# A two-layer attention trunk on one core: the product with the values turned round, with value pairs stationary, the transposed probabilities moving, and three float32r passes

## The chip, the core and the metric

The kernel runs on one core of a Trainium2 chip. The metric is the device time of one execution, in microseconds (us). Three runs of the kernel before took 888.66 to 889.86 us, with a median of 889.16 us.

## The reference, cut to what matters

The program is two layers over a sequence of 256 positions and 1024 columns. Each layer is a token mixer of three attention branches in parallel, followed by a SwiGLU network, each with a residual and a layer norm. The change touches only the last product of the three attentions:

```
p = softmax(logits)                       # per head: 256 queries x 256 keys, causal
o = p @ v                                 # v: 256 x 64 per head
ya, yb, yc: heads merged                  # 384, 256 and 384 columns
merged = sum_b gate_b * (y_b @ w_b)       # w_pa, w_pb, w_pc
```

The branches have 6, 4 and 6 heads here. The middle one is the dilated attention. It has three patterns of 4 heads, whose logits share one softmax for each of the 4 key-value heads, so that its probabilities are 3 groups that are added before the product with the values.

## The kernel before, in words

**Operands.** Everything is float32 in memory. For the large products each operand is split into a high part, rounded to float32r, and a low part, the rest, and the product is three passes: high by high, high by low, low by high. Weights arrive in pieces of up to 128x2048 in `raw`. ACT writes `w_hi` (L760) and DVE writes `w_lo` (L856). Activations are transposed by PE through an identity matrix, and ACT and DVE write the high and low part of the transposed tile out of PSUM (L764 and L861).

**One plan, five engines.** `write_plan` writes out one list of steps by hand. Every engine walks the whole list in order and issues its share of each step, so the order of the list is the order of each engine's queue. A weight product step is `mm` (L1040), 12 matmuls on a piece of 4 blocks. In the attention part, `attend` puts one half of an attention step behind each `mm`.

**Attention steps.** A unit is one pair of heads and one tile `t` of 128 queries. A layer has 16 units, in the order branch, pair, tile. `tick` k plans, in this order, the sum of the three groups of unit k-1 on POOL if that is dilated (L733, L734), the transposition of the probabilities of unit k-2 (`turn_p`, L1119, with ACT's copy to `prob_t` at L819), and the scores of unit k (L1099). DVE masks the scores and takes the maximum (L910 and L914), and ACT does the exponentials with their sums (L813). `half_tick` k, one `mm` later, plans the third group of scores of a dilated unit with t = 1 (`scores2`, L1099, L926) and the product with the values of unit k-2:

```
for e in range(2):
    h = 2 * u["p"] + e
    for j in range(u["t"] + 1):
        ins = pe.matmul(out[:, e * HEAD_DIM:(e + 1) * HEAD_DIM],
                        prob_t[:, e * w + j * P:e * w + (j + 1) * P],
                        values[g % 2][:, j, h * HEAD_DIM:(h + 1) * HEAD_DIM],
                        start=j == 0, stop=j == u["t"])
```

The transposed probabilities are stationary there, and 64 columns of values move (L1131), in plain float32. DVE then multiplies by the reciprocal of the sums and writes `y` (L934, L935). When a branch is complete, PE transposes `y` (L1055), and ACT and DVE split it for the projection `proj`.

**Queries, keys, values.** The step `spread` (L781) copies a finished block of the input product out of PSUM, on ACT: queries and keys to `stage`, values to `values`. For two branches POOL rotates the staged part (rope, L723 to L726) before PE transposes it (`turn_qk`, L1065). The forget gates of the first branch (`forget`, L877 to L890) need the third block, and `forget_sum` (L1075) on PE waits for them. Small transposed tiles alternate between two PSUM banks (`aux_bank`).

## Time and profile before

| | |
|---|---|
| median of 3 runs | 889.16 us |
| the profiled execution: its time | 889.12 us |
| its span | 887.3 us |
| PE busy | 842.2 us (95% of the span) |
| DVE busy | 511.1 us (58%) |
| ACT busy | 401.6 us (45%) |
| POOL busy | 48.9 us (6%) |
| chain that ended last | PE 84%, DVE 7%, ACT 3%, DMA 2%, POOL 2%, issue 1% |

The profile is of one execution. PE, DVE, ACT and POOL are the engines, PEld is PE's load of the stationary operand. In the trace's rows the first number is the start, the second the duration, both in us. Matmuls overlap one another, so what one costs is read from the distance of the starts. A float32 matmul leaves two records and a float32r matmul or a transposition one. The row of a stretch gives the stretch and its length, then PE, PEld, DVE, ACT and POOL busy with the number of instructions, PE's granted clock, the DMA share and GB/s. The row of a group gives its count, busy us and mean ns, then its idle time before it. A bracket at the end of a row is the time for which the engine sat idle before it, and what ended that.

### The profile page before, as it was taken

Reading aid. Unit: us, or ns where it says so; the run is one execution under the profiler, and the core shown is the slowest. Engines: PE = TensorE matmul, PEld = TensorE weight load, DVE = VectorE, ACT = ScalarE, POOL = GpSimd, SP = SyncE. Lnnn points to the kernel's source line nnn. Section 1 sums busy time; section 2 is a strip of 40 time slices with the busy share of each in tenths; the row PEclk is TensorE's granted clock in tenths of the full one; section 3 lists DMA queues with packets and bytes.
Section 4 is the critical chain, followed back from the end, with each engine's and each line's share of the span. In section 5 each row is a group of like instructions: output and inputs, shape, how many; then the busy total and the mean of one; then the engine's idle time right before and its main releaser. Section 6 shows DMA issues by size and latency. Waiting matters only on the chain.

```text
span 887.3 us, 10728 instructions
## 1 busy us (share of the span) xinstructions
PE 842.2 (95%) x4216; PEld 696.1 (78%) x4216; DVE 511.1 (58%) x728; ACT 401.6 (45%) x536; POOL 48.9 (6%) x86
## 2 busy tenths in 40 slices
PE   3989999999998999999999899999999899999995
PEld 2867888888886888888878678888888688888884
DVE  6564454636787545445685535554858765445436
ACT  3565455544444444344337554654444354344330
POOL 0012151000000000000000222300000000000000
PEclk9999999999999999999999999999999999999998
DMA  9573424456546864664437342434663675665601
GB/s 321 167 243 110 143 72 146 140 188 221 192 135 205 260 194 158 208 194 160 153 108 236 120 143 83 135 127 154 210 220 118 234 237 190 190 190 177 202 0 49
DMA packets 93458, 149.35 MB, mean 168 GB/s; under 512 B 3424, under 2 KB 52832, under 8 KB 93408
## 3 DMA queue, kind: packets, MB, share of 16 engines
q1 hardware_dynamic: 93408, 148.66, 51.4%
q8 instruction: 35, 0.57, 0.3%
q14 instruction: 15, 0.12, 0.0%
HBM read 147.60 MB, written 1.05 MB: 168 GB/s over the span
## 4 chain that ended last, share of the span: by engine, by line
PE 84%; DVE 7%; ACT 3%; DMA 2%; POOL 2%; issue 1%; SPq 0%; POOLq 0%; ACTq 0%; DVEq 0%
PE bank L1040 74%; PE bank L1055 3%; PE bank L1099 3%; DVE w_lo L856 2%; DMA raw<-in_w_in 2%; PE bank L1131 2%; ACT w_hi L760 1%; PE bank L1119 1%; PE bank L1065 1%; POOL rope_cos L723 1%; ACT shared L813 1%; DVE stats L973 1%; DVE x L1006 1%; DVE x L970 1%; DVE x L1003 1%
## 5 line engine op out<-in xcount | busy, mean ns | idle before, releaser
L856 DVE TENSOR_TENSOR w_lo<-raw,w_hi 128x2048 fp32r<-128x2048 f32 (+3 forms) x142 | 307.6, 2171 | 88.9 <-ACT w_hi L760 88.5
L1040 PE MATMUL bank<-w_hi,act_hi 128*128 128x512 f32 (+2 forms) x864 | 343.1, 397 | 3.4 <-DVE act_lo L861 3.4
L1040 PE MATMUL bank<-w_hi,act_lo 128*128 128x512 f32 (+2 forms) x864 | 333.5, 386 | 0.0
L1040 PE MATMUL bank<-w_lo,act_hi 128*128 128x512 f32 (+2 forms) x864 | 332.3, 385 | 0.0
L760 ACT CAST w_hi<-raw 128x2048 fp32r<-128x2048 f32 (+3 forms) x142 | 257.5, 1814 | 146.7 <-PE bank L1040 122.6
L1040 PEld LDWEIGHTS bank<-w_hi,act_hi 128*128 128x128 f32 x864 | 163.3, 189 | 33.0 <-DVE act_lo L861 3.8
L1040 PEld LDWEIGHTS bank<-w_hi,act_lo 128*128 128x128 f32 x864 | 162.8, 188 | 32.9
L1040 PEld LDWEIGHTS bank<-w_lo,act_hi 128*128 128x128 f32 x864 | 163.4, 189 | 28.7
L1040 PE MATMUL bank<-w_hi,y_hi 128*128 128x512 f32 x240 | 95.2, 397 | 0.0
L1040 PE MATMUL bank<-w_hi,y_lo 128*128 128x512 f32 x240 | 93.7, 391 | 0.0
L1040 PE MATMUL bank<-w_lo,y_hi 128*128 128x512 f32 x240 | 93.6, 390 | 0.0
L861 DVE TENSOR_TENSOR y_lo<-bank,y_hi 128x256 fp32r<-128x256 f32 (+1 forms) x56 | 23.3, 440 | 57.2 <-ACT y_hi L764 57.2
L1040 PEld LDWEIGHTS bank<-w_hi,y_lo 128*128 128x128 f32 x240 | 45.1, 188 | 9.5
L764 ACT CAST y_hi<-bank 128x256 fp32r<-128x256 f32 (+1 forms) x56 | 20.0, 387 | 71.9 <-PE bank L1055 71.9
L1040 PEld LDWEIGHTS bank<-w_hi,y_hi 128*128 128x128 f32 x240 | 45.1, 188 | 9.2
L1040 PEld LDWEIGHTS bank<-w_lo,y_hi 128*128 128x128 f32 x240 | 45.2, 188 | 8.8
L958 DVE TENSOR_TENSOR act_fn<-act_fn,bank 128x256 f32<-128x256 f32 x44 | 18.5, 421 | 58.2 <-ACT act_fn L829 56.5
L813 ACT ACTIVATE shared<-shared,neg_max 128x128 f32<-128x128 f32 (+3 forms) x64 | 33.8, 529 | 31.1 <-DVE neg_max L926 15.9
L829 ACT ACTIVATE act_fn<-bank 128x256 f32<-128x256 f32 x44 | 16.9, 384 | 61.8 <-PE bank L1040 61.8
L914 DVE CUSTOM_DVE_ANT_0 shared<-bank,tables 128x128 f32<-128x128 f32 (+1 forms) x48 | 15.3, 355 | 50.8 <-PE bank L1107 26.8
L723 POOL TENSOR_TENSOR rope_cos<-stage,tables 128x128 f32<-128x128 f32 (+1 forms) x16 | 11.3, 706 | 491.6 <-ACT stage L781 491.6
L869 DVE TENSOR_TENSOR qk_lo<-bank,qk_hi 128x512 fp32r<-128x512 f32 (+1 forms) x24 | 14.4, 602 | 41.4 <-ACT qk_hi L787 41.4
(88 smaller groups left out, 533.4 us busy)
## 6 DMA issues: line engine op xcount, KB each, us to landing
raw<-in_w_in SPq DMA_DIRECT2D x48, 1024.0 KB, 5.2
raw<-in_w_gate SPq DMA_DIRECT2D x44, 512.0 KB, 3.9
raw<-in_w_up SPq DMA_DIRECT2D x44, 512.0 KB, 5.0
raw<-in_w_down SPq DMA_DIRECT2D x22, 1024.0 KB, 5.0
raw<-in_w_o SPq DMA_DIRECT2D x8, 1024.0 KB, 5.3
raw<-in_w_in SPq DMA_DIRECT2D x4, 768.0 KB, 4.4
raw<-in_w_pa SPq DMA_DIRECT2D x4, 768.0 KB, 4.4
raw<-in_w_pc SPq DMA_DIRECT2D x4, 768.0 KB, 4.5
```

The source lines that it names most:

```text
L723: link(pool.tensor_tensor(rc, v, c4, ALU.mult))
L760: act.copy(weights(w_hi, i, HI_SLOTS), weights(raw, i, RAW_SLOTS)).then_inc(hi_done, 1)
L764: act.copy(hi[dst][:, dk:dk + nk, t * P:(t + 1) * P], group_view(bank[b], nk, P)).then_inc(turn_hi, 1)
L813: act.activation(pr, pr, ACT.Exp, bias=neg_max[:, slot:slot + 1], scale=-1.0, accum_out=denom[:, slot:slot + 1]).then_inc(exp_done, 1)
L829: act.activation(act_fn[2 * (c % 2) + t][:, 0:256], bank[b][:, 0:256], ACT.Silu).then_inc(silu_done, 1)
L856: dve.tensor_tensor(weights(w_lo, i, HI_SLOTS), weights(raw, i, RAW_SLOTS), weights(w_hi, i, HI_SLOTS).bitcast(F32), ALU.subtract).then_in ...
L861: dve.tensor_tensor(lo[dst][:, dk:dk + nk, t * P:(t + 1) * P], group_view(bank[b], nk, P), hi[dst][:, dk:dk + nk, t * P:(t + 1) * P].bitca ...
L958: dve.tensor_tensor(a[:, 256:512], a[:, 0:256], bank[b][:, 256:512], ALU.mult).then_inc(drained[b], 1)
L1040: ins = pe.matmul(bank[use[0]][:, 0:width], a, w[:, k, c0:c0 + width], start=start and k == 0 and p == 0, stop=stop and k == nk - 1 and p ...
L1055: ins = pe.transpose(out[:, k * P:(k + 1) * P], source(src, buf, k0 + k, t), ident)
L1099: ins = pe.matmul(bank[b][:, off:off + w], a[g % 2][rows, q, t * P:(t + 1) * P], k[g % 2][rows, K_PAIR[br] + pair, 0:w], start=p == 0, sto ...
L1131: ins = pe.matmul(out[:, e * HEAD_DIM:(e + 1) * HEAD_DIM], prob_t[:, e * w + j * P:e * w + (j + 1) * P], values[g % 2][:, j, h * HEAD_DIM: ...
```

## The change

The product with the values is planned once for a pair of heads, at its tile t = 1, and not once for each tile. The values of both heads (128 columns) are stationary, and the transposed probabilities of both heads and both tiles move: 512 columns for the first block of keys and 256 for the second. Values and probabilities are split into high and low parts, with three float32r passes for each block. The result comes out transposed, with both heads' values against both heads' probabilities. The two halves that belong together (`own_blocks`) are copied to `y_hi` by ACT and `y_lo` by DVE. The transposition of `y` goes away.

For this there are new steps. A step `weigh` on DVE, in the half tick behind the unit's exponentials, takes the reciprocal of the sums and multiplies the probabilities in place, and PE's `turn_p` now waits for it. DVE writes `prob_t_lo` in `turn_p`, ahead of the maxima of the same tick, and releases that bank. DVE writes `v_lo` in `spread`. Buffers of queries, keys and values are chosen by branch and not in rotation. The diff, cut to its core:

```
 PAIRS = [h // 2 for h in BRANCH_HEADS]
+ACT_SLOTS = [[0, 1, 2, 3], [4, 5, 6, 7]]
+Y_SLOTS = [[0, 1, 2], [3, 4], [5, 0, 1]]
                 plan.append(("sum", stage_of[k - 1]))
             if 0 <= k - 2 < len(units):
                 d = stage_of[k - 2]
-                d["pt"] = aux_bank()
+                d["pt"], d["pt_n"] = aux_bank(), count.next("pt")
...
             k = tick_at[0] - 1
             if 0 <= k < len(units) and stage_of[k]["b"] == 1 and stage_of[k]["t"]:
                 stage_of[k]["s2"] = [bank(4), bank(5)]
-                plan.append(("scores2", stage_of[k], g0 + 1))
-            if 0 <= k - 2 < len(units):
+                plan.append(("scores2", stage_of[k]))
+            if 0 <= k - 1 < len(units):
+                plan.append(("weigh", stage_of[k - 1]))
+            if 0 <= k - 2 < len(units) and stage_of[k - 2]["t"] == TT - 1:
                 d = stage_of[k - 2]
                 d["o"] = aux_bank()
-                plan.append(("values", d, g0 + d["b"]))
-                if d["p"] == PAIRS[d["b"]] - 1:
-                    last_y[d["b"], d["t"]] = d["o"]
-                    y_due.append((d["b"], d["t"]))
-
-        y_due = []
-        last_y = {}
+                plan.append(("values", d, count.next("values")))
+                for t in range(TT):
+                    y_turned[d["b"], t] = d["o"]
+
...
-            for b, t in due:
-                y_turned[b, t] = turn("y", 0, 0, BRANCH_KT[b], t, "y", 3 * ((g0 + b) % 2),
-                                      ("bank", last_y[b, t]))
-                    ev = dict(e=staged[0], b=b, pair=first, np=width // P, t=t, rope=b > 0, g=g0 + b, col=col)
-            plan.append(("spread", layer, c, t, use, segs, ev, g0))
+                    ev = dict(e=staged[0], b=b, pair=first, np=width // P, t=t, rope=b > 0)
+            v_n = count.next("v") if any(seg[0] == "v" for seg in segs) else 0
+            plan.append(("spread", c, t, use, segs, ev, v_n))
+            if c == 2:
+                forget_from[0] = v_n
             if ev is not None:
+                ev["staged"] = ("v", v_n) if v_n else ("bank", use)
...
-        values = [sb(f"values{s}", [P, TT, 384]) for s in range(2)]
+        shapes = [("ac", 384, 6), ("b", 256, 8)]
+        v_hi, v_lo = ([sb(f"v_{part}_{n}", [P, TT, width], F32R) for n, width, _ in shapes] for part in ("hi", "lo"))
-        prob_t = sb("prob_t", [P, 2 * SEQ])
-        y = sb("y", [P, TT, 384])
+        prob_t_hi, prob_t_lo = (sb(f"prob_t_{part}", [P, 3, 2 * P], F32R) for part in ("hi", "lo"))
...
+        def own_blocks(o):
+
+            return [(slice(e * HEAD_DIM, (e + 1) * HEAD_DIM),
+                     o[e * HEAD_DIM:(e + 1) * HEAD_DIM, :].rearrange("p (t e q) -> p t e q", t=TT, e=2)[:, :, e, :])
+                    for e in range(2)]
...
                         elif what == "v":
-                            out = values[(g0 + br) % 2][:, t, first:first + width]
+                            out = v_hi[br % 2][:, t, first:first + width]
                         ins = act.copy(out, src)
-                    ins.then_inc(drained[b], 1)
+                    ins.then_inc(v_hi_done if v_n else drained[b], 1)
...
                     u = step[1]
                     b, n = u["pt"]
                     act.wait_ge(filled[b], n)
-                    act.copy(prob_t[:, 0:2 * u["w"]], bank[b][:, 0:2 * u["w"]]).then_inc(drained[b], 1)
+                    t = u["t"]
+                    act.copy(prob_t_hi[:, t:2 * t + 1, :], group_view(bank[b], t + 1, 2 * P)
+                             ).then_inc(prob_t_hi_done, 1)
+                elif kind == "values":
+                    _, u, _ = step
+                    b, n = u["o"]
+                    act.wait_ge(filled[b], n)
+                    for rows, own_block in own_blocks(bank[b]):
+                        ins = act.copy(hi["y"][rows, Y_SLOTS[u["b"]][u["p"]], :].rearrange("p (t q) -> p t q", t=TT),
+                                       own_block)
+                    ins.then_inc(y_hi_done, 1)
...
                                       ALU.subtract).then_inc(drained[b], 1)
+                elif kind == "spread" and step[6]:
+                    _, c, t, (b, n), segs, ev, v_n = step
+                    dve.wait_ge(v_hi_done, v_n)
+                    for what, br, first, col0, width in segs:
+                        if what == "v":
+                            dve.tensor_tensor(v_lo[br % 2][:, t, first:first + width], bank[b][:, col0:col0 + width],
+                                              v_hi[br % 2][:, t, first:first + width].bitcast(F32),
+                                              ALU.subtract).then_inc(drained[b], 1)
                 elif kind == "forget":
 
-                    _, layer, (fb, fn) = step
+                    _, layer, v_n = step
                     dve.wait_ge(tables_loaded, 48)
-                    dve.wait_ge(drained[fb], fn)
+                    dve.wait_ge(v_hi_done, v_n)
                     link(dve.tensor_tensor(f_in[:, :, :], f_in[:, :, :],
...
                                                  dil_mask[:, 2, :], -SCALE, nm, ALU.add, ALU.min,
                                                  nm).then_inc(drained[b], 1)
+                elif kind == "weigh":
+
+                    u = step[1]
+                    s0 = 2 * (u["u"] % 4)
+                    if u["b"] == 1:
+                        dve.wait_ge(summed, u["sum_n"])
+                    else:
+                        dve.wait_ge(exp_done, 2 * u["u"] + 2)
+                    link(dve.reciprocal(rdenom[:, s0:s0 + 2], denom[:, s0:s0 + 2]))
+                    for e in range(2):
+                        pr = prob[u["t"]][e][:, 0:u["w"]]
+                        ins = dve.tensor_scalar(pr, pr, rdenom[:, s0 + e:s0 + e + 1], None, ALU.mult)
+                    ins.then_inc(weighed, 1)
+                elif kind == "turn_p":
+                    u = step[1]
+                    b, n = u["pt"]
+                    t = u["t"]
+                    dve.wait_ge(prob_t_hi_done, u["pt_n"])
+                    dve.tensor_tensor(prob_t_lo[:, t:2 * t + 1, :], group_view(bank[b], t + 1, 2 * P),
+                                      prob_t_hi[:, t:2 * t + 1, :].bitcast(F32),
+                                      ALU.subtract).then_inc(drained[b], 1)
                 elif kind == "values":
-                    u = step[1]
+                    _, u, y_n = step
                     b, n = u["o"]
-                    s0, h0 = 2 * (u["u"] % 4), 2 * u["p"] * HEAD_DIM
-                    dve.wait_ge(filled[b], n)
-                    link(dve.reciprocal(rdenom[:, s0:s0 + 2], denom[:, s0:s0 + 2]))
-                    dve.tensor_tensor(y[:, u["t"], h0:h0 + 2 * HEAD_DIM].rearrange("p (e c) -> p e c", e=2),
-                                      group_view(bank[b], 2, HEAD_DIM),
-                                      rdenom[:, s0:s0 + 2].unsqueeze(2).broadcast_to([P, 2, HEAD_DIM]),
-                                      ALU.mult).then_inc(drained[b], 1)
+                    k = Y_SLOTS[u["b"]][u["p"]]
+                    dve.wait_ge(y_hi_done, y_n)
+                    for rows, own_block in own_blocks(bank[b]):
+                        by_t = [m["y"][rows, k, :].rearrange("p (t q) -> p t q", t=TT) for m in (lo, hi)]
+                        ins = dve.tensor_tensor(by_t[0], own_block, by_t[1].bitcast(F32), ALU.subtract)
+                    ins.then_inc(drained[b], 1)
...
                 elif kind == "turn_p":
                     u = step[1]
-                    if u["b"] == 1:
-                        pe.wait_ge(summed, u["sum_n"])
-                    else:
-                        pe.wait_ge(exp_done, 2 * u["u"] + 2)
+                    pe.wait_ge(weighed, u["u"] + 1)
-                    w = u["w"]
-                    for e in range(2):
-                        for j in range(u["t"] + 1):
-                            ins = pe.transpose(out[:, e * w + j * P:e * w + (j + 1) * P],
-                                               prob[u["t"]][e][:, j * P:(j + 1) * P], ident)
+                    for j in range(u["t"] + 1):
+                        for e in range(2):
+                            c0 = (2 * j + e) * P
+                            ins = pe.transpose(out[:, c0:c0 + P], prob[u["t"]][e][:, j * P:(j + 1) * P], ident)
                     ins.then_inc(done, 1)
                 elif kind == "values":
-                    _, u, g = step
+
+                    _, u, _ = step
                     pb_, pn = u["pt"]
                     pe.wait_ge(drained[pb_], pn)
                     out, done = take(u["o"])
-                    w = u["w"]
-                    for e in range(2):
-                        h = 2 * u["p"] + e
-                        for j in range(u["t"] + 1):
-                            ins = pe.matmul(out[:, e * HEAD_DIM:(e + 1) * HEAD_DIM],
-                                            prob_t[:, e * w + j * P:e * w + (j + 1) * P],
-                                            values[g % 2][:, j, h * HEAD_DIM:(h + 1) * HEAD_DIM],
-                                            start=j == 0, stop=j == u["t"])
+                    pair = slice(u["p"] * P, (u["p"] + 1) * P)
+                    for j in range(TT):
+                        cols = slice(j * 2 * P, 4 * P)
+                        for p, (v, pt) in enumerate(((v_hi, prob_t_hi), (v_hi, prob_t_lo), (v_lo, prob_t_hi))):
+                            moving = pt[:, 2 * j:2 + j, :].rearrange("p a q -> p (a q)")
+                            ins = pe.matmul(out[:, cols], v[u["b"] % 2][:, j, pair], moving,
+                                            start=j == 0 and p == 0, stop=j == TT - 1 and p == 2)
                     ins.then_inc(done, 1)
```

The first place is DVE's queue in the middle of the dilated branch. Units are counted from 0 in a layer: unit 5 is the first branch's last, units 6 and 7 are the dilated pair 0 at t = 0 and t = 1, and unit 8 is pair 1 at t = 0. Before, from behind the third group's maxima of unit 7 (`scores2`) to behind the `w_lo` after the maxima of unit 8:

```order
L934 RECIPROCAL rdenom<-denom 128x2 [waits filled6]
L935 TENSOR_TENSOR y<-bank,rdenom 128x128 [waits dve_own]
L910 ISA shared,neg_max<-bank,tables 128x384 [waits filled4]
L910 ISA shared,neg_max<-bank,tables 128x384 [waits filled5]
L861 TENSOR_TENSOR y_lo<-bank,y_hi 128x3x128 [waits turn_hi]
L856 TENSOR_TENSOR w_lo<-raw,w_hi 128x2048 [waits hi_done]
L934 RECIPROCAL rdenom<-denom 128x2 [waits filled7]
L935 TENSOR_TENSOR y<-bank,rdenom 128x128 [waits dve_own]
```

The same stretch now, up to the `weigh` of unit 7 (the last two rows), for which the `turn_p` of unit 7 waits on PE:

```order
L971 RECIPROCAL rdenom<-denom 128x2 [waits summed]
L974 TENSOR_SCALAR shared<-shared,rdenom 128x128 [waits dve_own]
L991 TENSOR_TENSOR y_lo<-bank,y_hi 64x256 [waits y_hi_done]
L991 TENSOR_TENSOR y_lo<-bank,y_hi 64x256
L981 TENSOR_TENSOR prob_t_lo<-bank,prob_t_hi 128x256 [waits prob_t_hi_done]
L944 ISA shared,neg_max<-bank,tables 128x384 [waits filled4]
L944 ISA shared,neg_max<-bank,tables 128x384 [waits filled5]
L903 TENSOR_TENSOR v_lo_ac<-bank,v_hi_ac 128x384 [waits v_hi_done]
L882 TENSOR_TENSOR w_lo<-raw,w_hi 128x2048 [waits hi_done]
L971 RECIPROCAL rdenom<-denom 128x2 [waits summed]
L974 TENSOR_SCALAR shared<-shared,rdenom 128x256 [waits dve_own]
L974 TENSOR_SCALAR shared<-shared,rdenom 128x256
```

In the new queue there stand `y_lo` of unit 5, `prob_t_lo` of unit 6 and `v_lo`, and each waits for ACT. The maxima of unit 8 and a `w_lo` of 2048 stand behind them and ahead of the `weigh` of unit 7. The reciprocal and multiply behind the product, and `y_lo` of a transposition, are gone.

ACT's queue over the same stretch, before, from the exponentials of unit 7:

```order
L813 ACTIVATE shared,denom<-shared,neg_max 128x768 [waits drained4]
L813 ACTIVATE shared,denom<-shared,neg_max 128x768 [waits drained5]
L760 CAST w_hi<-raw 128x2048 [waits piece_used,raw_full1]
L819 COPY prob_t<-bank 128x256 [waits filled7]
L813 ACTIVATE shared,denom<-shared,neg_max 128x384 [waits drained4]
L813 ACTIVATE shared,denom<-shared,neg_max 128x384 [waits drained5]
L764 CAST y_hi<-bank 128x3x128 [waits filled6]
L781 COPY values<-bank 128x384 [waits filled2]
L781 COPY values<-bank 128x384 [waits filled3]
```

And now:

```order
L829 ACTIVATE shared,denom<-shared,neg_max 128x768 [waits drained4]
L829 ACTIVATE shared,denom<-shared,neg_max 128x768 [waits drained5]
L843 CAST y_hi<-bank 64x256 [waits filled6]
L843 CAST y_hi<-bank 64x256
L776 CAST w_hi<-raw 128x2048 [waits piece_used,raw_full1]
L836 CAST prob_t_hi<-bank 128x256 [waits filled7]
L829 ACTIVATE shared,denom<-shared,neg_max 128x384 [waits drained4]
L829 ACTIVATE shared,denom<-shared,neg_max 128x384 [waits drained5]
L797 CAST v_hi_ac<-bank 128x384 [waits filled2]
L797 CAST v_hi_ac<-bank 128x384 [waits filled3]
```

ACT has the same work here but for `y_hi`: it stands ahead of the piece's `w_hi` and in two parts, where it stood behind the exponentials of unit 8 in one. The copy of the probabilities still stands behind that `w_hi`. DVE's `prob_t_lo` now waits for this copy.

## Rows read from the trace of the kernel before

**Rows 1.** Busy time by engine in the attention part of layer 1 (windows)
```profile
63.00:196.00 133.00, 128.64 (x753) 106.74 (x751) 64.67 (x135) 68.20 (x126) 24.03 (x40) 1.00 0.40 127
```
**Rows 2.** Groups by line, PE: the transpositions of the staged queries and keys
```profile
L1065 PE MATMUL bank<-tables,stage 128*128 128x128 f32 x80 | 13.5, 283 | 8.7 <-POOL stage L726 8.7
```

**Rows 3.** Timeline, PE: the product with the values of a unit with t = 1
```profile
151.84 0.39 PE L1040 MATMUL bank<-w_hi,act_lo 128*128 128x512 f32 x1
152.07 1.00 PE L1131 MATMUL bank<-values,prob_t 128*128 128x64 f32 x8
...
153.19 0.39 PE L1040 MATMUL bank<-w_lo,act_hi 128*128 128x512 f32 x1
```

**Rows 4.** Timeline, PE: float32r matmuls of 256 columns; a transposition of y
```profile
56.15 0.28 PE L1075 MATMUL bank<-upper_r,logf_lo 128*128 128x256 f32 x1
56.27 0.22 PE L1077 MATMUL bank<-upper_r,logf_hi 128*128 128x128 f32 x1
...
195.20 0.39 PE L1040 MATMUL bank<-w_hi,act_lo 128*128 128x512 f32 x1
195.44 0.49 PE L1055 MATMUL bank<-tables,y 128*128 128x128 f32 x3
...
196.00 0.39 PE L1040 MATMUL bank<-w_lo,act_hi 128*128 128x512 f32 x1
```

**Rows 5.** Timeline, PE: the longest staged wait, and turn_p of unit 7
```profile
114.56 0.66 PE L1065 MATMUL bank<-tables,stage 128*128 128x128 f32 x4 [1.62 <-POOL stage L726]
...
132.40 0.60 PE L1119 MATMUL bank<-tables,shared 128*128 128x128 f32 x4
```

**Rows 6.** Timeline, DVE: from the third maxima of unit 7
```profile
123.19 0.48 DVE L926 CUSTOM_DVE_ANT_0 shared<-bank,tables,neg_max 128x256 f32<-128x256 f32 x1
...
126.81 0.56 DVE L910 CUSTOM_DVE_ANT_1 shared<-bank,tables 128x384 f32<-128x384 f32 x1 [2.34 <-PE bank L1099]
...
129.32 0.56 DVE L861 TENSOR_TENSOR y_lo<-bank,y_hi 128x384 fp32r<-128x384 f32 x1 [1.46 <-ACT y_hi L764]
129.79 2.28 DVE L856 TENSOR_TENSOR w_lo<-raw,w_hi 128x2048 fp32r<-128x2048 f32 x1
131.99 0.16 DVE L934 RECIPROCAL rdenom<-denom 128x2 f32<-128x2 f32 x1
132.18 0.29 DVE L935 TENSOR_TENSOR y<-bank,rdenom 128x128 f32<-128x128 f32 x1
```

**Rows 7.** Timeline, ACT: the same stretch
```profile
123.70 0.94 ACT L813 ACTIVATE shared<-shared,neg_max 128x768 f32<-128x768 f32 x1 [3.51 <-DVE neg_max L926]
...
125.56 1.89 ACT L760 CAST w_hi<-raw 128x2048 fp32r<-128x2048 f32 x1
127.35 0.36 ACT L819 COPY prob_t<-bank 128x256 f32<-128x256 f32 x1
127.61 0.61 ACT L813 ACTIVATE shared<-shared,neg_max 128x384 f32<-128x384 f32 x1
...
128.82 0.46 ACT L764 CAST y_hi<-bank 128x384 fp32r<-128x384 f32 x1
129.18 0.85 ACT L781 COPY values<-bank 128x384 f32<-128x384 f32 x2
```

**Rows 8.** Timeline, DVE and POOL: the forget gates' start; two POOL additions
```profile
50.22 0.42 DVE L869 TENSOR_TENSOR qk_lo<-bank,qk_hi 128x256 fp32r<-128x256 f32 x1 [0.89 <-ACT qk_hi L787]
50.56 2.28 DVE L856 TENSOR_TENSOR w_lo<-raw,w_hi 128x2048 fp32r<-128x2048 f32 x1
...
129.00 0.73 POOL L733 TENSOR_TENSOR shared<-shared 128x256 f32<-128x256 f32 x1 [0.61 <-ACT shared L813]
129.81 2.86 POOL L734 TENSOR_TENSOR shared<-shared 128x256 f32<-128x256 f32 x1
```

**Rows 9.** Timeline, PE: the first large product's start
```profile
17.66 0.80 PE L1040 MATMUL bank<-w_hi,act_hi 128*128 128x512 f32 x1 [3.42 <-DVE act_lo L861]
```

**Rows 10.** Chain of waits, its part there: start, us, what
```profile
17.66 7.54 PE bank L1040 x24
```

71 lines of the change are left out of this document (38 added, 33 removed).

## The prediction

> **What bounds the kernel now.** I read the page's shares first, then the busy time by stretch, the chain of waits, and the timeline of PE with every idle time in it. In the attention part of a layer PE is busy for 128.6 of 133 us, and DVE and ACT for half of it [rows 1]. PE goes from matmul to matmul there, so a PE instruction taken out is time gained, except in front of a wait. All waits of PE in that part are for the staged queries and keys, 8.7 us in 8 places in both layers [rows 2], the longest 1.62 us [rows 5]. DVE and ACT have slack in sum. Whether they have it at each place must be read from their queues, since both work strictly in the order of the plan.
>
> **The change on PE.** A product for t = 1 takes the start of the second matmul behind it less that of the last one before it, less two normal distances of 0.23 us: 153.19 - 151.84 - 0.46 = 0.89 us for 8 records [rows 3]. The product for t = 0 has 4 records, so 0.45 us. The new product for a pair is three matmuls of 512 columns at 0.23 us and three of 256. For these the distance is 0.12 us [rows 4], which makes 0.69 + 0.36 = 1.05 us. So each of the 8 places with t = 1 in a layer grows by 0.16 us, 1.3 us in all. Each of the 8 places with t = 0 gives up 0.45 us. But three of these eight stand right in front of a `turn_qk` that waits for the rope. There PE only waits longer, and so 5 x 0.45 = 2.25 us count. The transpositions of y, 16 of 128x128 in a layer: three of them alone take 196.00 - 195.20 - 0.46 = 0.34 us [rows 4], 0.11 us each. Beside other transpositions the changeover is shared, so I take 0.10 us each, 1.6 us. PE's sum for a layer is +1.3 - 2.25 - 1.6 = **-2.6 us**.
>
> **Small delays in front of PE's waits.** (a) The forget gates. DVE gets `v_lo` of 128 columns once before and once behind the `w_lo` that precedes the gates. The distance behind a PSUM difference of 256 columns is 0.34 us [rows 8], and 0.22 us is the estimate for 128. The chain to `forget_sum`, for which PE waits already, grows by 2 x 0.22 = 0.4 us. (b) In two of the three rope places, `prob_t_lo` of 128x256 stands between the scores and their maxima, behind which come ACT's exponentials, the copy to `stage`, and the rope. The maxima move by about 0.15 us, so +0.3 us. (c) A POOL addition of 0.73 us takes 2.86 us where it starts with a DVE `w_lo`, and ends 0.6 us behind it [rows 8]. POOL and DVE exclude each other there. The new multiplication of `weigh` follows such a `w_lo` just where POOL rotates. No row shows a wide multiplication by a scalar. Its bounds are nothing on one side and, for two at 0.29 us as the old multiply of 128 columns [rows 6] and a bit more for 256, 0.7 us on the other. I take 0.2 us at each of three places, nearer to the lower bound, since POOL has a lock of its own at the time: +0.6 us. Sum of a, b and c: **+1.3 us** for a layer.
>
> The Trainium skill, "SBUF — State Buffer", § Practical consequences, says that a DVE tensor_scalar in its two-port mode shuts POOL out fully, and so does an instruction with two SBUF inputs. The trace agrees for the second (2.86 against 0.73 us), and no run here shows the first. By that rule (c) would be up to the whole multiplication.
>
> **The queue in the dilated branch.** This term decides the sign. I follow unit 7 with the durations of the trace, its first layer's clock, and the new order of the two queues. The `turn_p` of unit 7 starts at 132.40 now [rows 5].
> - The third maxima of unit 7 stand at 123.19 [rows 6]. Ahead of them `prob_t_lo` of 512 columns comes in (0.62) and a `y_lo` of 384 goes (0.47), and PE is 0.15 later by its longer products. So they start 0.3 later and the exponentials run from 123.97 for 1.86 us [rows 7], to 125.83.
> - ACT then has `y_hi` in two parts. They are bounded by the distance behind a copy of 256 columns in 128 partitions, 0.26 each, and by its duration, 0.36 [rows 7]. I take 0.55 in all: 126.4. Then `w_hi`, 1.8 to the next start [rows 7]: 128.2. Then the copy of unit 6's probabilities, 0.36: 128.55.
> - DVE waited for this and writes `prob_t_lo`: 128.95. Only now come the maxima of unit 8, which stand at 126.81 before [rows 6]. The first ends at 129.55, and two exponentials at 0.61 [rows 7] end at 130.8.
> - ACT's first `v_hi` takes 0.43 (two in 0.85) [rows 7]: 131.2. DVE's `v_lo` of 384, 0.47 [rows 6]: 131.7. Then `w_lo`, which has to run ahead of `weigh`, 2.2 [rows 6]: 133.9. Before, it started at 129.79.
> - `weigh` of unit 7: reciprocal 0.2 to the next [rows 6] and two multiplications of 256 columns, bounded by 0.16 each, as the reciprocal of 2 columns [rows 6], and by 0.42, as a difference of 256 [rows 8]. I take 0.3, between the two: 134.7, or 134.4 to 135.0. PE sees it at 134.8.
> - PE comes to this `turn_p` at 132.40 + 0.15 + 0.16 for the product of unit 5 - 0.28 - 0.28 for two turns of y - 0.45 for unit 6's product = 131.7. It waits **3.1 us**, 2.8 to 3.3 by the bounds.
>
> The page "VectorE: DVE Perf Modes" of the Trainium skill, § The perf-mode tier table, gives 1227 ns for a float32 tensor_scalar of 2048 columns. An estimate from it for 256 columns is 0.15 us, and with it the wait would be 2.8 us. No row here shows it.
>
> Behind this wait PE is late, so ACT and DVE have caught up. I walked the other ticks of a layer in the same way: each `weigh` is over 0.3 to 2.4 us before its `turn_p`, and each `prob_t_lo` 0.5 to 2 us before its product. The new work on DVE (32 `prob_t_lo`, 16 `v_lo`, 32 `y_lo` of 64 partitions, 64 multiplications, less 32 old multiplies and 12 `y_lo`) is thereby hidden behind PE's matmuls. If that cover were gone, it would cost its delay at each tick. `w_lo` runs several pieces ahead of its use, and its delay of 2 to 4 us reaches no `mm`. The weights' DMAs wait for `w_lo` of three pieces before and shift with it, at a share of 0.40 [rows 1]. I cost them at nothing.
>
> **Sum.** A layer: -2.6 + 1.3 + 3.1 = +1.8 us. Two layers: +3.7 us with the rounding. Against the profiled execution's own 889.12 us this is 892.8 us. The median shown, 889.16 us, is the same within 0.1 us.
>
> **The rivals.**
> - *PE's saving comes through whole, no long wait.* The walk hangs on ACT's and DVE's exact order. If one link is shorter, such as `w_hi` off the path since its piece is late or early, the `turn_p` is met in time. For it: both engines are idle half of the time [rows 1]. Against it: the order of the queues is printed, and all its durations have rows. Then 889.12 + 2 x (-2.6 + 1.3) = 886.5 us, faster. It decides where the chain is shorter by 3 us. Chance 0.25.
> - *PE falls to the lower clock behind the new wait.* At the start, behind an idle time of 3.42 us [rows 9], 24 matmuls took 7.54 us [rows 10] and not 24 x 0.23 = 5.5 us, 2.0 us more. A distance of 0.43 us for 512 columns is 1.2 GHz and 0.23 us goes with 2.4 GHz. The waits in front of the rope, 1.62 us at the longest [rows 5], did nothing of the kind. The new one, 3.1 us, is near the first. Then 892.8 + 2 x 2.0 = 896.8 us. Chance 0.15. The Trainium skill's "TensorE: Matmul & The Clock Gate", § HAM oscillation, says that idle stretches between bursts bring the slower level back. The trace agrees for the start, and no row shows it for 3.1 us.
> - *`weigh` and the rope exclude each other in full,* 0.7 us at six places in place of 0.2: 892.8 + 3.0 = 895.8 us. Chance 0.1.
> - *Small waits at ticks that I took as just met,* three or four of 0.5 us in a layer: 892.8 + 3.5 = 896.3 us. Against it: each has some slack. Chance 0.1.
> - *The change doesn't do what it says:* six records for a pair must stand on PE for the 12 before. Its order shows them, so no chance is kept for it.
>
> **How the numbers follow.** Forecast 0.40, with 891 to 894.5 us as its own range. The bounds take 0.6 us off or 0.5 us on at the wait, and (c) 1.2 us off or 3 us on. The range has to hold both signs: from 886.0, a little under the first rival, to 897.5, above the second. What a measurement of this kernel can tell from no change is about 0.2%, 1.8 us, so 887.4 to 890.9 us is no difference. Faster comes from the first rival, 0.23 of its 0.25. Same is the rest of it and a wait of only half the length, 0.17. Slower is the remainder, 0.60.
>
> **What would show it.** In the profile after: PE's idle time ahead of the `turn_p` of the dilated branch, released by DVE's multiplication, about 3 us once in each layer, and nowhere else; the product's places at 1.05 us; staged waits of more than 8.7 us in sum, by 6 x 0.45 and a bit; POOL's rope rows longer where a multiplication runs. The prediction is wrong if that `turn_p` finds no wait, or if waits for DVE or ACT stand at many ticks. It is also wrong if the new float32r matmuls are farther apart than 0.23 and 0.12 us.

## The result, and the profile after

The changed kernel took 902.66 us (median of 4 runs, 901.75 to 902.95) beside 889.15 us for the kernel before. The ratio is 1.015, with a 95% interval of 1.0132 to 1.0167. It is slower, as forecast, but by 13.5 us and not by 3.7 us, and 902.66 us lies outside the range of 886.0 to 897.5 us.

| | before | after |
|---|---|---|
| median | 889.15 us | 902.66 us |
| the profiled execution: time, span | 889.12, 887.3 us | 901.75, 900.0 us |
| PE busy | 842.2 us | 841.3 us |
| DVE busy | 511.1 us | 547.4 us |
| ACT busy | 401.6 us | 410.0 us |
| PE's mean granted clock | 0.997 | 0.988 |

From the page of the changed kernel, the busy times:

```profile
PE 841.3 (93%) x4088; PEld 689.5 (77%) x4088; DVE 547.4 (61%) x828; ACT 410.0 (46%) x556; POOL 51.6 (6%) x86
```

PE is busy for about as long as before, though it has less to do. The missing time is idle time and matmuls at a lower clock. PE's waits (who waits, for whom; us in total, times, longest):

```profile
PE bank L1119 <- POOL stage L742: 14.4, 8, 2.0
PE bank L1170 <- DVE shared L974: 7.1, 2, 3.5
...
PE bank L1129 <- DVE logf_lo L924: 3.0, 2, 1.5
```

The staged waits, those of `turn_qk` for POOL's rotation, are 14.4 us where they were 8.7 [rows 2]. They stand at four places in each layer, the rope places, counted here in order of time. In layer 1 PE waited there for 1.46, 1.13, 0.15 and 1.62 us before, and waits for 1.48, 1.67, 2.04 and 2.03 us now. At the second and the fourth the growth, 0.54 and 0.41 us, is about the 0.45 us of the product that is saved in front of them. The `turn_p` of unit 7 (L1170) waits for 3.5 us in each layer, and no other `turn_p` waits. PE's timeline in layer 1, with the third rope place, a product, and the `turn_p` of unit 7:

```profile
99.26 0.44 PE L1119 MATMUL bank<-tables,stage 128*128 128x128 f32 x2 [2.04 <-POOL stage L742]
...
99.91 0.63 PE L1094 MATMUL bank<-w_lo,act_hi 128*128 128x512 f32 x1
100.33 0.63 PE L1094 MATMUL bank<-w_hi,act_lo 128*128 128x512 f32 x1
...
108.10 0.39 PE L1183 MATMUL bank<-prob_t_hi,v_hi_ac 128*128 128x512 f32 x1
...
108.78 0.28 PE L1183 MATMUL bank<-prob_t_hi,v_hi_ac 128*128 128x256 f32 x1
108.89 0.28 PE L1183 MATMUL bank<-prob_t_lo,v_hi_ac 128*128 128x256 f32 x1
...
109.13 0.40 PE L1094 MATMUL bank<-w_hi,act_hi 128*128 128x512 f32 x1
...
139.01 0.66 PE L1170 MATMUL bank<-tables,shared 128*128 128x128 f32 x4 [3.55 <-DVE shared L974]
...
141.08 0.63 PE L1094 MATMUL bank<-w_lo,act_hi 128*128 128x512 f32 x1
141.51 0.63 PE L1094 MATMUL bank<-w_hi,act_lo 128*128 128x512 f32 x1
```

The product's distances are as forecast, 0.12 us for 256 columns and 1.03 us for a pair (109.13 - 108.10). Behind both waits, matmuls of 512 columns stand 0.43 us apart and not 0.23: PE's clock has fallen to 1.2 GHz. This is called a fall below. The windows behind them show it (the number before the DMA share is the granted clock, 1.00 over the attention part before [rows 1]):

```profile
101.00:107.00 6.00, 6.00 (x31) 4.71 (x31) 1.49 (x6) 2.84 (x5) 0.95 (x4) 0.83 0.31 121
139.00:145.00 6.00, 5.99 (x28) 4.59 (x28) 4.00 (x7) 0.59 (x1) 0.00 (x0) 0.72 0.54 176
575.00:581.00 6.00, 5.48 (x23) 4.35 (x24) 4.38 (x9) 0.59 (x1) 0.05 (x1) 0.51 0.55 175
```

By the distance of the same two matmuls before and after, each fall costs about 1.6 us (103.88 - 99.26 = 4.62 us where 3.05 us stood), and 7.2 us the four together. The one behind the `turn_p` of layer 2 costs 2.4 us: there the clock was low when the wait ended, and the four transpositions took 1.11 us and not 0.66. Behind the 2.03 us at the fourth rope place, as long as the wait at the third, there is no fall.

**Where a layer's time went.** The changed kernel falls behind the old one by 5.7 us in layer 1 and 6.8 us in layer 2, where +1.8 us was forecast. Over the forecast are the wait at the third rope place (2.04 us for 0.15; 0.45 of that is the product saved in front of it and 0.35 were forecast, so 1.1 too much), the lower clock behind it (1.6), the wait at `turn_p` (0.45 over the 3.1) and the lower clock behind that (1.6 and 2.4). That makes 4.8 and 5.6 us. So 0.9 and 0.6 us of what was forecast did not come, most of it (b) and (c), which had 0.55 us at the other rope places, where the growth was at most 0.1 us more than the product saved.

**Why the third rope place waits for 2 us.** POOL's and DVE's timelines of the changed kernel there:

```profile
96.33 0.32 POOL L739 TENSOR_TENSOR rope_cos<-stage,tables 128x64 f32<-128x64 f32 x1 [10.79 <-ACT stage L797]
96.73 1.75 POOL L740 TENSOR_TENSOR rope_sin<-stage,tables 128x64 f32<-128x64 f32 x1
98.56 0.32 POOL L741 TENSOR_TENSOR stage<-rope_cos,rope_sin 128x32 f32<-128x32 f32 x1
```

```profile
96.22 0.42 DVE L903 TENSOR_TENSOR v_lo_b<-bank,v_hi_b 128x256 fp32r<-128x256 f32 x1 [1.26 <-ACT stage L797]
96.56 1.75 DVE L882 TENSOR_TENSOR w_lo<-raw,w_hi 128x1536 fp32r<-128x1536 f32 x1
98.22 0.16 DVE L971 RECIPROCAL rdenom<-denom 128x2 f32<-128x2 f32 x1
98.42 0.62 DVE L974 TENSOR_SCALAR shared<-shared,rdenom 128x256 f32<-128x256 f32 x2
```

And the two rows of the kernel before, one of each engine:

```profile
94.07 1.75 DVE L856 TENSOR_TENSOR w_lo<-raw,w_hi 128x1536 fp32r<-128x1536 f32 x1
```

```profile
96.08 0.32 POOL L724 TENSOR_TENSOR rope_sin<-stage,tables 128x64 f32<-128x64 f32 x1
```

Before, the rotation began at 95.53 and met only the last 0.3 us of `w_lo`. Now `v_lo` stands ahead of `w_lo` and waits 1.26 us for ACT's `v_hi`. So `w_lo` starts in the middle of the rotation, and POOL's second multiplication lasts until 0.17 us behind the end of `w_lo`: 1.75 us for 0.32. It is the exclusion of rows 8, but by the moved `w_lo`, and not by `weigh`'s multiplication, to which term (c) gave it.

At the other three rope places the rotation met a `w_lo` before the change too. At the second its first multiplication, 0.46 us elsewhere, took this long in the kernel before and in the changed one:

```profile
78.69 1.20 POOL L723 TENSOR_TENSOR rope_cos<-stage,tables 128x128 f32<-128x128 f32 x1 [9.11 <-ACT stage L781]
```

```profile
79.23 1.20 POOL L739 TENSOR_TENSOR rope_cos<-stage,tables 128x128 f32<-128x128 f32 x1 [9.27 <-ACT stage L797]
```

### The profile page after: what moved, and what is told of

It is laid out like the page before. It is cut to its first block, busy times and chain, and to the rows that moved or that the text cites. A ratio compares the mean times of both kernels' runs of the same rounds, so it can differ in the third digit from the quotient of the medians.

```text
span 900.0 us, 10564 instructions
## 1 busy us (share of the span) xinstructions
PE 841.3 (93%) x4088; PEld 689.5 (77%) x4088; DVE 547.4 (61%) x828; ACT 410.0 (46%) x556; POOL 51.6 (6%) x86
## 3 DMA queue, kind: packets, MB, share of 16 engines
HBM read 147.60 MB, written 1.05 MB: 165 GB/s over the span
## 4 chain that ended last, share of the span: by engine, by line
PE 79%; DVE 9%; ACT 6%; DMA 2%; POOL 2%; issue 2%; SPq 0%; POOLq 0%; ACTq 0%; DVEq 0%
PE bank L1094 71%; DVE w_lo L882 3%; DMA raw<-in_w_in 2%; ACT w_hi L776 2%; PE bank L1109 2%; PE bank L1153 2%; PE bank L1183 2%; ACT shared L829 1%; PE bank L1170 1%; PE bank L1119 1%; POOL rope_cos L739 1%; POOL rope_sin L740 1%; ACT stage L797 1%; DVE stats L1027 1%; DVE x L1060 1%
## 5 line engine op out<-in xcount | busy, mean ns | idle before, releaser
L981 DVE TENSOR_TENSOR prob_t_lo<-bank,prob_t_hi 128x256 fp32r<-128x256 f32 (+1 forms) x32 | 17.9, 558 | 56.9 <-ACT prob_t_hi L836 56.7
L780 ACT CAST y_hi<-bank 128x256 fp32r<-128x256 f32 x44 | 14.8, 375 | 70.7 <-PE bank L1109 70.7
L887 DVE TENSOR_TENSOR y_lo<-bank,y_hi 128x256 fp32r<-128x256 f32 x44 | 17.1, 420 | 36.0 <-ACT y_hi L780 36.0
L780 ACT CAST act_hi<-bank 128x512 fp32r<-128x512 f32 x24 | 13.9, 589 | 36.0 <-PE bank L1109 36.0
```

The costliest lines, as they stand in the source:

```text
L780: act.copy(hi[dst][:, dk:dk + nk, t * P:(t + 1) * P], group_view(bank[b], nk, P)).then_inc(turn_hi, 1)
L887: dve.tensor_tensor(lo[dst][:, dk:dk + nk, t * P:(t + 1) * P], group_view(bank[b], nk, P), hi[dst][:, dk:dk + nk, t * P:(t + 1) * P].bitca ...
L981: dve.tensor_tensor(prob_t_lo[:, t:2 * t + 1, :], group_view(bank[b], t + 1, 2 * P), prob_t_hi[:, t:2 * t + 1, :].bitcast(F32), ALU.subtra ...
```

## The experiments

In all of them only the order of steps on DVE, or on ACT and POOL, is changed, unless something else is said.

**`w_lo` ahead of `v_lo` at the third rope place.** The edit as it stands in DVE's queue:

```
 L948 ISA neg_max 128x1
+L882 TENSOR_TENSOR w_lo<-raw,w_hi 128x1536
 L903 TENSOR_TENSOR v_lo_b<-bank,v_hi_b 128x256
-L882 TENSOR_TENSOR w_lo<-raw,w_hi 128x1536
 L971 RECIPROCAL rdenom<-denom 128x2
```

> The changed kernel with one exchange on DVE in each layer: at the third rope place the w_lo of 1536 columns runs ahead of v_lo, as before the change. Theory (v_lo, which waits for ACT's v_hi, pushed that w_lo onto POOL's rotation, which then stood still until w_lo ended): w_lo starts at about 94.95 and not at 96.56 us, POOL's second rope multiplication takes about 0.32 and not 1.75 us, PE's wait there falls from 2.04 to about 0.85 us, and PE's clock no longer falls behind it (1.57 us a layer). Together -2 x (1.2 + 1.57) = -5.5 us: 897.1 us. Rival 1 (the lower clock behind that place has nothing to do with the wait): 902.7 - 2.4 = 900.3 us. Rival 2 (weigh's multiplications hold POOL there, as my term c had it): the wait stays over 1.6 us and the time at 902.7 us.

Measured: 898.89 us (895.4 to 899.9). In its PE and POOL timelines:

```profile
98.44 0.44 PE L1119 MATMUL bank<-tables,stage 128*128 128x128 f32 x2 [0.70 <-POOL stage L742]
```

```profile
96.85 0.48 POOL L739 TENSOR_TENSOR rope_cos<-stage,tables 128x64 f32<-128x64 f32 x1 [10.79 <-ACT stage L797]
97.40 0.32 POOL L740 TENSOR_TENSOR rope_sin<-stage,tables 128x64 f32<-128x64 f32 x1
```

The rotation again meets only the end of `w_lo` (0.48 us for its first multiplication, as before the change), the wait is 0.70 us, and the clock does not fall behind it, in either layer. The theory of the wait holds and rival 2 is out: `weigh` still runs right there. Of the 5.5 us 3.8 came in the median. In the profiled run the clock now fell elsewhere: 0.72 in the 6 us behind the fourth rope place of layer 2, which waits for 2.01 us in both kernels, and 0.54 behind unit 7's `turn_p` in layer 1, where it was 0.72. So that run, at 899.28 us, got back the wait alone. The one at 895.4 us has a mean clock of 0.993 and not 0.988.

**`weigh` of unit 7 ahead of `v_lo` and `w_lo`.** In DVE's queue:

```
 L944 ISA neg_max 128x1
+L971 RECIPROCAL rdenom<-denom 128x2
+L974 TENSOR_SCALAR shared<-shared,rdenom 128x256 x2
 L903 TENSOR_TENSOR v_lo_ac<-bank,v_hi_ac 128x384
 L882 TENSOR_TENSOR w_lo<-raw,w_hi 128x2048
-L971 RECIPROCAL rdenom<-denom 128x2
-L974 TENSOR_SCALAR shared<-shared,rdenom 128x256 x2
```

> The changed kernel with one move on DVE in each layer: the weigh of unit 7 runs right behind the maxima of unit 8, ahead of v_lo and w_lo. Theory (that queue makes PE's wait of 3.55 us at the turn_p of unit 7, and the wait makes the lower clock behind it, 1.6 us in layer 1 and 2.4 in layer 2): no wait at that turn_p, no matmuls at the lower clock there: 902.7 - 7.1 - 4.1 = 891.5 us. Rival 1 (the lower clock has another cause and stays): 895.6 us. Rival 2 (PE only waits a few matmuls later, since all is late there): the PE idle time appears at another step within 10 us, and the time is over 898 us.

Measured: 890.51 us (10 runs, 889.8 to 892.67), ratio to the kernel before 1.0015 (1.0005 to 1.0025). The wait at that `turn_p` is gone, and so is the lower clock, as its window shows. What is new is a wait of 0.8 us in all for the maxima (rival 2 in small). One queue position cost 12 us in the medians, 90% of the loss. At its own place the traces account for 7.1 + 4.0 - 0.8 = 10.3 us of that. In this profiled run the clock did not fall behind the third rope places either, though PE's waits there, 2.04 and 2.05 us, were as long as before; why, the runs don't show.

```profile
139.00:145.00 6.00, 5.38 (x34) 4.15 (x32) 4.29 (x14) 3.09 (x7) 1.09 (x1) 1.00 0.85 285
```

**PE kept busy in the two waits.**

```
+                    out, done = take(u["pt"])
+                    for _ in range(26 if u["b"] == 1 and u["p"] == 0 and u["t"] else 0):
+                        pe.matmul(out[:, 0:SEQ], upper_r[:, 0:P], upper_r[:, :], start=True, stop=True)
                     pe.wait_ge(weighed, u["u"] + 1)
-                    out, done = take(u["pt"])
```

The same stands, with 14, in `turn_qk` of the third rope place.

> The changed kernel with PE kept busy in its two new waits: 14 extra float32r matmuls of 256 columns (1.7 us) ahead of the wait at the third rope place and 26 (3.1 us) ahead of the wait at the turn_p of unit 7. Their results are overwritten by the transpositions behind them. The waits end when they ended. Theory (the idle time itself takes the clock down): granted clock stays at 1.0, the stretches behind both waits run at 0.23 us for 512 columns, and 7.2 us come back: 895.5 us. Rival (the slow stretch comes from something else in that place, for instance late operands or a collision with DVE): time within 1 us of 902.7.

Measured: 897.06 us (895.1 to 897.54). The stretches behind both filled waits run at the full clock. At unit 7, where the clock fell behind every unfilled wait of 2.87 us or more, this shows the idle time as the cause. At the third rope place it is weaker evidence, since in the run above the clock stayed up there with the wait unfilled. And 5.6 of the 7.2 us came back: the profiled run shows a fall in a new place, behind the wait for the forget gates. It was 1.71 us; nothing fell behind it in the other kernels, where it was 1.66 us at most:

```profile
58.62 0.39 PE L1131 MATMUL bank<-upper_r,logf_hi 128*128 128x256 f32 x1 [1.71 <-DVE logf_lo L924]
```

```profile
58.00:64.00 6.00, 5.38 (x22) 4.09 (x24) 3.35 (x5) 5.39 (x5) 0.00 (x0) 0.72 0.42 139
102.00:108.00 6.00, 6.00 (x36) 4.85 (x36) 2.22 (x7) 4.14 (x8) 1.16 (x4) 1.00 0.53 175
140.00:146.00 6.00, 5.93 (x39) 4.58 (x40) 4.79 (x11) 0.79 (x2) 0.00 (x0) 1.00 0.54 175
```

**No multiplications in `weigh`.** The reciprocal releases PE, and the probabilities stay unnormalised:

```
-                    link(dve.reciprocal(rdenom[:, s0:s0 + 2], denom[:, s0:s0 + 2]))
-                    for e in range(2):
-                        pr = prob[u["t"]][e][:, 0:u["w"]]
-                        ins = dve.tensor_scalar(pr, pr, rdenom[:, s0 + e:s0 + e + 1], None, ALU.mult)
-                    ins.then_inc(weighed, 1)
+                    dve.reciprocal(rdenom[:, s0:s0 + 2], denom[:, s0:s0 + 2]).then_inc(weighed, 1)
```

> The changed kernel without weigh's 64 multiplications: the probabilities go into the product unnormalised; only the reciprocals are left. Theory (the multiplications don't hold POOL; they only stand in DVE's chain to the turn_p of unit 7): the staged waits stay at 14.4 us within 0.5, POOL's rope rows stay (1.75 us at the third place), the wait of unit 7's turn_p falls from 3.55 to about 2.7 us, time 902.7 - 1.7 = 901.0 us. Rival (term c: the multiplications and the rope exclude each other, 0.2 to 0.7 us at six places): staged waits 12 us or less, time 897 to 900 us.

Measured: 901.94 us (897.79 to 902.04). PE's waits:

```profile
PE bank L1115 <- POOL stage L742: 14.3, 8, 2.0
PE bank L1166 <- DVE rdenom L971: 4.9, 2, 2.6
```

Staged waits of 14.3 us without any multiplication: term (c) is at most 0.1 us in all, and what was forecast for it was a term too many. The waits of unit 7 are 2.29 and 2.62 us, down as expected, but the median is only 0.7 us less. The profiled run is the fastest of the four, at a mean clock of 0.991 with three falls; the others have 0.986.

**`prob_t_lo` behind the maxima, in every tick.**

```
+        if plan[i][0] == "turn_p" and plan[i + 1][0] == "scores":
+            plan[i], plan[i + 1] = plan[i + 1], plan[i]
```

> The changed kernel with DVE's prob_t_lo behind the maxima of the same tick in every tick. Theory (the chain to the weigh of unit 7 runs through ACT's copy of the probabilities, prob_t_lo and only then the maxima of unit 8): those maxima start some 1.5 us earlier, the wait at the turn_p of unit 7 falls from 3.55 to about 2.0 us, the staged waits fall by no more than 0.2 us at two places (term b). Time 902.7 - 2 x 1.7 = 899.3 us, 895 to 900 as the lower clock comes or not behind a wait of 2.0 us. Rival (the exponentials of unit 8 wait for something else, such as ACT's w_hi): the wait stays at 3.5 us and the time over 901.5 us.

Measured: 899.41 us (899.16 to 902.89). The wait of unit 7 is 2.51 us in both layers, 1.0 us less and not 1.5. So `prob_t_lo` is a link of the chain, as the walk had it, but behind it `v_lo` still waits for ACT's `v_hi`. The staged waits did not fall but rose to 15.1 us, so term (b) is not shown. The trace tells why. At the second rope place POOL's first multiplication meets `w_lo` and ends 0.31 us behind it, whenever it starts, here at 80.38 and in the changed kernel at 80.43 (79.23 + 1.20):

```profile
78.85 1.53 POOL L739 TENSOR_TENSOR rope_cos<-stage,tables 128x128 f32<-128x128 f32 x1 [9.11 <-ACT stage L797]
```

`prob_t_lo` now stands between the maxima and that `w_lo`, which therefore starts at 77.79 for 77.83, while PE is there 0.24 us sooner. So PE waits longer, 1.85 us for 1.67.

**Both exchanges, third place and unit 7, together.** DVE's loop over the steps:

```
-            for step in PLAN:
+            for step in weigh_ahead(v_lo_behind_w_lo(PLAN), lambda u: u["b"] == 1 and u["p"] == 0 and u["t"]):
```

> Both exchanges at once: w_lo ahead of v_lo at the third rope place, and weigh of unit 7 ahead of v_lo and w_lo. Theory (the two waits with their lower clock are all that lies between the forecast without a long wait and the measured time): no wait over 1.0 us at the third place, none over 0.7 at the turn_p, time 902.7 - 3.8 (measured for the one) - 12.2 (for the other) = 886.7; with 890.5 - 2 x 1.35 it is 887.8. I expect 887.3 us, which is 2 us faster than the kernel before. Rival (PE's work for the new product was not less by 2.6 us a layer): 889 us or more.

Measured: 887.63 us (10 runs, 885.9 to 888.37), ratio 0.998 (0.9971 to 0.9989). It is within 0.4 us of what was expected, and a little faster than the kernel before. This is the first rival of the prediction, 886.5 us, brought about by the two moves. The runs at 886 us have a mean clock of 0.997, those at 888.4 us one of 0.993. One of these was profiled, and it has a fall behind the fourth rope place (2.02 us) in each layer.

**The copies of `spread` and the rotation early.** From the fourth block on, ACT and POOL do them right behind the matmuls that fill the bank, ahead of the tick's copy of the probabilities and its exponentials:

```
+        if step[0] == "spread" and step[1] > 2:
+            j = i - 1
+            while plan[j][0] != "mm":
+                j -= 1
+            plan.insert(j + 1, plan.pop(i))
```

> The changed kernel with ACT's and POOL's share of spread (the copies out of PSUM, the rotation) right behind the matmuls that fill the bank, ahead of the tick's copy of probabilities and exponentials; DVE as it is. Theory (the staged waits hang on ACT's queue, and beside it on w_lo, which holds POOL): the rotations start 1.5 to 2 us earlier, at the third place it ends before w_lo starts, at the other three it still meets w_lo. Staged waits 14.4 -> about 5 us, wait at unit 7's turn_p 3.55 -> about 2 us since v_lo no longer waits. Time 902.7 - 9.4 - 3.1 - 3.2 (clock, third place) = 887 us; 885 to 891. Rival (the rotation only stands still longer behind DVE): staged waits over 10 us, time over 894 us.

Measured: 883.39 us (882.7 to 884.41). This is 1.6 us under the range that was expected. The staged waits are 1.8 us in all and not 5. The wait of unit 7's `turn_p` stays at 2.87 us, where 2 were expected, and the clock falls behind it. POOL at the second rope place, where PE still waits 0.90 us:

```profile
76.75 2.31 POOL L741 TENSOR_TENSOR stage<-rope_cos,rope_sin 128x64 f32<-128x64 f32 x1
```

It still meets `w_lo`: 2.31 us for 0.32.

**In addition, every `weigh` ahead of `w_lo`.** The move of unit 7 for all units, on DVE:

```
+        if step[0] == "weigh" and chosen(step[1]):
+            j = i - 1
+            while plan[j][0] not in ("scores", "turn_p"):
+                j -= 1
+            if plan[j][0] == "scores":
+                plan.insert(j + 1, plan.pop(i))
```

> The kernel with the early spread of the last one and, on DVE, every weigh right behind the maxima and ahead of w_lo, so that the rotation is over before w_lo starts. Theory (all of the staged waits and the wait of unit 7 hang on the order of ACT's and DVE's queues, and PE has less work than before): staged waits under 2 us in all, no wait at a turn_p, no lower clock in the attention part: 902.7 - 13 - 7.1 - 7.2 = 875.4 us, 873 to 880. Rival (the delayed w_lo now makes PE wait at an mm): PE idle time in front of a large product of over 0.5 us, time over 880 us.

Measured: 873.72 us, and 873.62 us when it was run again; ratio 0.9824 (0.9809 to 0.9838). No staged wait and no wait at a `turn_p` is left. At the second rope place (DVE, then POOL):

```profile
76.48 0.84 DVE L974 TENSOR_SCALAR shared<-shared,rdenom 128x256 f32<-128x256 f32 x2
77.24 2.28 DVE L882 TENSOR_TENSOR w_lo<-raw,w_hi 128x2048 fp32r<-128x2048 f32 x1
```

```profile
76.44 0.32 POOL L741 TENSOR_TENSOR stage<-rope_cos,rope_sin 128x64 f32<-128x64 f32 x1
76.85 0.32 POOL L742 TENSOR_TENSOR stage<-rope_cos,rope_sin 128x64 f32<-128x64 f32 x1
```

The rotation ends 0.07 us before `w_lo` starts, and beside the multiplication it keeps its pace.

**The early spread in the kernel before.** On POOL and ACT, with nothing else changed:

```
-            for step in PLAN:
+            for step in spread_ahead(PLAN):
```

> The kernel before (product not turned round) with the same early spread on ACT and POOL. It tells what of the gain belongs to the order of the queues and what to the turned product. Theory (the staged waits of 8.7 us go to about 1 us, nothing else changes; without these waits all eight products for t = 0 of a layer count): 889.3 - 7.7 = 881.6 us, so 8 us slower than the turned kernel with its queues put right (873.7). Of these 8 us I can account for 2 x (2.6 + 3 x 0.45) = 7.9 us less PE work and about 1 us of staged waits, less 0.4 us in front of the forget gates and 1.9 us in front of scores. Rival (the turned product saves nothing, and w_lo behind weigh was the whole of the gain): 875 us or less.

Measured: 879.92 us (ratio 0.9895), 1.7 us faster than expected. So of the 15.6 us between the kernel before and the one above, 9.4 belong to the order of the queues and could be had without turning the product. The other 6.2 us are the turned product's. The kernel above has 1.3 us more waits (1.9 for scores and 2.8 for forget gates, beside 1.2 staged and 2.2 for forget gates here), so PE's work is less by 7.5 us, 3.75 us a layer. The forecast's own terms make 3.95 when all eight products for t = 0 count: the PE part of the prediction was right to 0.2 us.

**The maxima first in addition,** on DVE, to early spread and `weigh` ahead:

```
-            for step in weigh_ahead(PLAN, lambda u: True):
+            for step in maxima_first(weigh_ahead(PLAN, lambda u: True)):
```

> The turned kernel with early spread and weigh ahead of w_lo, and DVE's prob_t_lo behind the maxima in every tick. Theory (PE's last waits, 0.96 us in each layer in front of the third group's scores of unit 9, end with the maxima, which then come 0.6 us sooner): 873.7 - 1.3 = 872.4 us. Rival (prob_t_lo later makes the product wait, or pushes w_lo onto the rotation as in the run with the maxima first): 874.5 us or more.

Measured: 874.1 us (873.74 to 875.57), no gain. It is the rival's mechanism, at 0.4 us under its time. The wait for the maxima is gone, and one of 1.19 us has come at the second rope place:

```profile
77.67 2.28 DVE L882 TENSOR_TENSOR w_lo<-raw,w_hi 128x2048 fp32r<-128x2048 f32 x1
```

```profile
77.11 0.48 POOL L741 TENSOR_TENSOR stage<-rope_cos,rope_sin 128x64 f32<-128x64 f32 x1
77.67 2.45 POOL L742 TENSOR_TENSOR stage<-rope_cos,rope_sin 128x64 f32<-128x64 f32 x1
```

Against the rotation, `w_lo` comes 0.23 us earlier than in the kernel above, and POOL's addition before the last took 0.48 us and not 0.32, since a multiplication had begun first. So POOL's last addition started together with `w_lo`, and lasted until 0.17 us behind its end.

**The maxima first in the dilated branch alone, and `v_lo` behind the forget gates.** In DVE's queue at the gates, beside the exchange in the dilated ticks:

```
-L903 TENSOR_TENSOR v_lo_ac<-bank,v_hi_ac 128x128
-L882 TENSOR_TENSOR w_lo<-raw,w_hi 128x2048
-L903 TENSOR_TENSOR v_lo_ac<-bank,v_hi_ac 128x128
+L882 TENSOR_TENSOR w_lo<-raw,w_hi 128x2048
 L911 TENSOR_TENSOR f_in<-f_in,f_bias 128x12
...
 L924 TENSOR_TENSOR logf_lo<-neg_logf,logf_hi 128x8x6
+L903 TENSOR_TENSOR v_lo_ac<-bank,v_hi_ac 128x128 x2
```

> The turned kernel with early spread and weigh ahead of w_lo; beside that, on DVE, the maxima ahead of prob_t_lo in the dilated branch alone, and both v_lo of the third block behind the forget gates. Theory (term a, two v_lo of 0.2 us each in DVE's chain to the forget gates, is what PE's wait there grew by, and the second rope place, which the run with all maxima first spoiled, is left alone): the waits in front of the forget sum fall from 2.8 to about 2.1 us in both layers, those in front of the scores of unit 9 from 1.9 to about 0.6: 873.7 - 0.7 - 1.3 = 871.7 us. Rival (the v_lo only move in front of the next piece of that chain): 873 us or more.

Beside it ran the kernel with the early spread once more:

> The kernel with early spread and weigh ahead of w_lo once more, beside the last one on the same chip: 873.7 us again, within 0.5.

Measured: 870.93 us (869.92 to 871.33), ratio 0.9788 (0.9773 to 0.9803), beside 873.62 us for the repeated one. It is the fastest version, 2.1% under the kernel before and 3.5% under the change as it was made. Of PE's waits in the attention part these are left, the first shorter by 0.5 us:

```profile
PE bank L1129 <- DVE logf_lo L924: 2.3, 2, 1.3
...
PE bank L1153 <- DVE cum_row L930: 1.4, 1, 1.4
PE bank L1153 <- issue: 1.4, 1, 1.4
```

## Why the prediction was wrong, and where it was right

- **The wait of unit 7: right in kind, a little short.** It was forecast at 3.1 us, 2.8 to 3.3 by its bounds, and measured at 3.55 and 3.54 us, above them. DVE's rows there, in the changed kernel:

```profile
132.57 0.43 DVE L981 TENSOR_TENSOR prob_t_lo<-bank,prob_t_hi 128x256 fp32r<-128x256 f32 x1 [1.48 <-ACT prob_t_hi L836]
...
135.20 0.56 DVE L903 TENSOR_TENSOR v_lo_ac<-bank,v_hi_ac 128x384 fp32r<-128x384 f32 x1 [1.26 <-ACT v_hi_ac L797]
135.68 2.28 DVE L882 TENSOR_TENSOR w_lo<-raw,w_hi 128x2048 fp32r<-128x2048 f32 x1
137.88 0.16 DVE L971 RECIPROCAL rdenom<-denom 128x2 f32<-128x2 f32 x1
138.07 0.88 DVE L974 TENSOR_SCALAR shared<-shared,rdenom 128x256 f32<-128x256 f32 x2
```

  By the third maxima of unit 7 (127.10 here, 123.19 before, 0.3 of it forecast) the kernel is 3.6 us late there. Less that, the first four rows stand at 128.97, 131.60, 132.08 and 134.28, and the walk has them at 128.55, 131.2, 131.7 and 133.9: every link is there. The walk was 0.4 us short before the first one (`y_hi` took 0.75 us and not 0.55, `w_hi` 1.9 and not 1.8), and the two multiplications took 0.88 us and not 0.6. They take 0.62 us where POOL is idle. Here POOL's addition for unit 8, held by the `w_lo` from 135.69 to 138.54, still ran. The 0.15 us for one multiplication that the prediction names beside its 0.3 was half of that.
- **"PE falls to the lower clock behind the new wait", chance 0.15: this is the step that failed.** The prediction named it, priced it at 2.0 us a layer and took it for unlikely, since waits of 1.62 us had done nothing, and left it out of the sum. Measured: 1.6 and 2.4 us behind that wait. Behind all six waits from 2.87 to 3.55 us in these runs the clock fell. That two times 2.0 us is also the sum of 1.6 and 2.4 is luck, for the start [rows 9, 10] shows no fall: PE was at the lower clock there before the wait of 3.42 us. Its first four transpositions took 1.09 us, where four at the full clock take 0.60 [rows 5] and the four at the lower one above took 1.11. In the kernel before:

```profile
11.77 1.09 PE L1055 MATMUL bank<-tables,x 128*128 128x128 f32 x4 [11.77 <-DVE x L1006]
```

  So nothing in the trace of before could tell what a wait of 3.1 us does.
- **The third rope place: the second step that failed.** The sum gave it +0.35 us, by (b) and (c). I asked what each new DVE step delays behind it on the path to PE, and for `v_lo` only at the forget gates and at unit 7. The prediction costed the delay of `w_lo` "at nothing", since it "reaches no `mm`". That `v_lo` moves such a `w_lo` onto POOL's rotation, for which PE does wait, I did not ask. It cost 1.1 us over the forecast and then took the clock down, 1.6 us more, in both layers.
- **Term (c): wrong.** The multiplications cost the rotation nothing that PE sees. Term (a), 0.4 us, was +0.2 and +0.4. Term (b) could not be found by itself; at three of the four rope places the end of `w_lo` sets when POOL's rotation goes on.
- **PE's work: right.** 1.03 us for a pair (1.05), and 3.75 us less for a layer where nothing waits (3.95).
- **The rival without a long wait** gives about the time that was then measured with both waits taken away, 886.5 us for 887.6, with what falls of the clock are left there.

The two failed steps hang together. With the third place at 0.9 us and the clock term counted behind unit 7, the forecast's own sum is 896.8 us, inside the range. Two more falls, behind the third rope places (3.1 us), and waits there that are 2.2 us longer took it beyond. What decides whether the clock falls behind a wait of about 2 us stays open.

## What to carry to other kernels

When a new instruction that waits is put into a strict queue, follow what it pushes back, also when that is on nobody's path: here a `w_lo` with slack landed on POOL's rotation and stopped it. Count a PE wait at its length and a fall of the clock (1.6 us) besides, by these runs with a chance of about a half at 2 us and as good as surely from 2.9 us. And before a change of the arithmetic is judged, let each queue do first what another engine waits for: the same product was 1.5% slower or 2.1% faster by the order of some steps, and the old product gained 1.0% by such an order too.
